# Token stage of a hybrid attention and MLP layer on one core: rope tables in one piece ahead of the token tiles, the first weights' low part on VectorE, norm vectors and rope rows loaded sooner

## What is computed

```python
def modulate(x, g, shift, scale):
    return rmsnorm(x, g) * (1.0 + scale) + shift

def project(h, w_in, g_q_a, w_uq, g_kv_a, w_ukv, g_mla_q, g_mla_k, g_swa_q, g_swa_k, rope):
    z = h @ w_in
    cq, ckv, kr, qs, ks, vs = jnp.split(z, offs, axis=-1)
    q_m = (rmsnorm(cq, g_q_a) @ w_uq).reshape(B, n, MLA_HEADS, MLA_QK)
    kv = (rmsnorm(ckv, g_kv_a) @ w_ukv).reshape(B, n, MLA_HEADS, MLA_NOPE + MLA_V)
    ...
    if rope is not None:
        q_m = jnp.concatenate([q_m[..., :MLA_NOPE], apply_rope(q_m[..., MLA_NOPE:], cos_m, sin_m)], axis=-1)
        k_m = jnp.concatenate([k_m[..., :MLA_NOPE], apply_rope(k_m[..., MLA_NOPE:], cos_m, sin_m)], axis=-1)
        q_s = apply_rope(q_s, cos_s, sin_s)
        k_s = apply_rope(k_s, cos_s, sin_s)
    return q_m, k_m, v_m, q_s, k_s, v_s
```

## Time and profile before

| | before |
|---|---|
| three runs, median (lowest to highest) | 1425.94 us (1423.24 to 1425.99) |
| the profiled execution's own time | 1423.98 us |
| its span in the trace | 1422.2 us |
| PE busy over the span | 95% |
| DVE, ACT, POOL busy over the span | 67%, 49%, 34% |
| mean granted TensorE clock | 0.989 of full speed |

### The profile page before, as it was taken

One profiled execution on the slowest core, in us unless ns is written; L12 is line 12 of the kernel. 1 busy time (PEld: TensorE's weight loads), 2 busy tenths in 40 slices (PEclk: granted clock), 3 DMA queues, 4 the chain that ended last, 5 costly groups with the idle time before them and its releaser, 6 DMA issues.

```text
span 1422.2 us, 18829 instructions
## 1 busy us (share of the span) xinstructions
PE 1354.3 (95%) x7274; PEld 1144.6 (80%) x7274; DVE 959.3 (67%) x1327; ACT 703.0 (49%) x1339; POOL 479.5 (34%) x295
## 2 busy tenths in 40 slices
PE   5799997999999999999999999999999999999969
PEld 1588886888788998998888888888888888888857
DVE  1888776888877877785774646557465656637477
ACT  2656655777778776972223424333233324323321
POOL 2666563000099992501002304132140503223060
PEclk9899999999999999999999999999999999999989
DMA  9465657900146556201123112121210212121003
GB/s 376 153 176 167 163 170 253 279 1 1 51 169 204 182 145 188 69 1 45 45 65 128 30 30 89 30 74 30 89 30 15 89 30 76 29 89 30 30 29 119
DMA packets 116969, 141.33 MB, mean 99 GB/s; under 512 B 7672, under 2 KB 98680, under 8 KB 114064
## 3 DMA queue, kind: packets, MB, share of 16 engines
q1 hardware_dynamic: 116624, 140.08, 31.5%
q0 software_dynamic: 256, 0.05, 0.0%
HBM read 108.37 MB, written 31.74 MB: 99 GB/s over the span
## 4 chain that ended last, share of the span: by engine, by line
PE 75%; DVE 11%; ACT 9%; DMA 2%; issue 2%; SPq 0%; DVEq 0%; ACTq 0%
PE f_ps L2024 24%; PE f_ps L2259 21%; PE a_ps L1381 7%; PE o_ps L1736 6%; PE a_ps L1397 6%; PE a_ps L1425 5%; ACT s_pr L1476 3%; PE t_ps L943 2%; ACT s_pT L1486 2%; PE t_ps L932 2%; DMA t_wm<-in_w_mod 1%; DVE s_nmx L1559 1%; PE t_ps L958 1%; ACT l_pr L1493 1%; DVE l_nb L1564 1%
## 5 line engine op out<-in xcount | busy, mean ns | idle before, releaser
L2024 PE MATMUL f_ps<-h,f_w 128*128 128x512 f32 x1536 | 357.9, 389 | 0.4 <-DVE h L1802 0.3
L2024 PEld LDWEIGHTS f_ps<-h,f_w 128*128 128x128 f32 x1536 | 288.1, 188 | 60.7 <-DVE h L1802 0.7
L2186 DVE TENSOR_TENSOR mix<-mix,f_ps 128x512 f32<-128x512 f32 x208 | 136.3, 683 | 149.6 <-PE f_ps L2259 149.6
L2067 POOL TENSOR_TENSOR f_w<-f_w,f_g 128x1024 f32<-128x1024 f32 x32 | 81.8, 2577 | 393.2 <-DMA f_w<-in_w_mlp 345.8
L2259 PE MATMUL f_ps<-f_bh,f_ah 128*128 128x512 f32 x448 | 175.4, 391 | 13.2 <-DVE mix L2186 13.1
L2259 PE MATMUL f_ps<-f_bh,f_al 128*128 128x512 f32 x448 | 175.0, 391 | 0.0
L2259 PE MATMUL f_ps<-f_bl,f_ah 128*128 128x512 f32 x448 | 175.0, 391 | 0.0
L2104 ACT ACTIVATE f_a<-f_ps 128x512 f32<-128x512 f32 x64 | 38.2, 597 | 254.7 <-PE f_ps L2024 254.7
L1573 DVE TENSOR_TENSOR l_pT<-a_ps,l_pT 128x512 fp32r<-128x512 f32 (+1 forms) x192 | 109.0, 594 | 53.0 <-ACT l_pT L1486 52.9
L1381 PE MATMUL a_ps<-l_k,l_q 96*128 96x512 f32 (+1 forms) x576 | 136.4, 366 | 0.5 <-DVE l_mo L1594 0.5
L943 PE MATMUL t_ps<-w_in,t_h 128*128 128x416 f32 (+2 forms) x600 | 123.6, 351 | 0.0
(11 more groups left out here) (212 smaller groups left out, 2355.2 us busy)
## 6 DMA issues: line engine op xcount, KB each, us to landing
l_wg<-in_w_mod SPq DMA_DIRECT2D x8, 2048.0 KB, 8.5
f_w1r<-in_w_mlp SPq DMA_DIRECT2D x32, 512.0 KB, 4.1
f_w<-in_w_mlp SPq DMA_DIRECT2D x16, 1024.0 KB, 5.0
t_wm<-in_w_mod SPq DMA_DIRECT2D x8, 1024.0 KB, 12.7
scratch_k<-t_kT SPq DMA_DIRECT2D x20, 384.0 KB, 4.3
l_k<-scratch_k SPq DMA_DIRECT2D x8, 960.0 KB, 9.7
scratch_q<-t_qT SPq DMA_DIRECT2D x16, 384.0 KB, 5.0
l_q<-scratch_q SPq DMA_DIRECT2D x8, 768.0 KB, 6.6
```

The costliest lines, as they stand in the source:

```text
L2024: last = nc.tensor.matmul(ps[:, b, :], w1[:, g % 2, w, k, :], h2[x][:, k, half * HB:(half + 1) * HB], start=(k == 0 and i == 0), stop=(k = ...
L2186: V.tensor_tensor(y, x, ps[:, bank_of(d, i, t), :].rearrange("p (k c) -> p k c", c=P), ALU.add).then_inc(added, 1)
```

## The change

Four things move. (1) On SP the two transfers of the norm vectors (`cols`, 2.5 KB, and `norms`, 160 KB) go ahead of the last two modulation blocks, and the rope rows (768 KB) go ahead of kv, r0 and r1. (2) On DVE the three small operations that scale the gains go from behind `scale_x(1)` to ahead of the bias. (3) The low part of a0 goes from POOL to DVE, ahead of `modulate_first`. (4) All four table blocks go ahead of POOL's loop.

```diff
@@ sync
         load_x(0)
+        sp.dma_start(cols[:, :], A["norm_cols"]).then_inc(gains, 16)
+        sp.dma_start(norms[:, :], A["norm_rows"]).then_inc(gains, 16)
         load_wm(KC - 2)
         load_wm(KC - 1)
         load_raw("a0")
         load_x(1)
         load_raw("a1")
-        sp.dma_start(cols[:, :], A["norm_cols"]).then_inc(gains, 16)
-        sp.dma_start(norms[:, :], A["norm_rows"]).then_inc(gains, 16)
+        sp.dma_start(rope[:, :, :], A["rope_rows"]).then_inc(rope_loaded, 16)
         load_raw("kv")
         load_raw("r0")
         load_raw("r1")
-        sp.dma_start(rope[:, :, :], A["rope_rows"]).then_inc(rope_loaded, 16)
@@ gpsimd
-        pool.wait_ge(w_hi, 1)
-        G.tensor_tensor(split_view("a0", 1), raw_view("a0"), split_view("a0", 0).bitcast(F32), ALU.subtract).then_inc(first_low, 1)
         pool.wait_ge(gains, 32)
         G.tensor_copy(tab[:, 0, 64:96], b_mk[:, NOPE:QK])
         link(G.tensor_copy(tab[:, 0, 256:320], b_sk))
+        pool.wait_ge(rope_loaded, 16)
+        pool.wait_ge(gains_scaled, 1)
+        build_table(0, 64, ROPE, b_mk[:, NOPE:QK])
+        build_table(2 * ROPE, 256, SD, b_sk)
+        build_table(2 * ROPE, 128, SD, b_sq)
+        build_table(0, 0, ROPE, b_mq[:, NOPE:QK])
         for i in range(NT + 1):
...
-            if i == 0:
-                pool.wait_ge(rope_loaded, 16)
-                build_table(0, 64, ROPE, b_mk[:, NOPE:QK])
-            if i == 1:
-                pool.wait_ge(gains_scaled, 1)
-                build_table(2 * ROPE, 256, SD, b_sk)
...
@@ vector
         inverse_x(0)
+        dve.wait_ge(gains, 32)
+        dve.wait_ge(cleared, 7)
+        V.scalar_tensor_tensor(out=g_qk[0:NOPE, :], in0=cols[0:NOPE, 3:4], scalar=MLA_SCALE, in1=cols[0:NOPE, 4:5],
+                               op0=ALU.mult, op1=ALU.mult)
+        V.tensor_scalar(b_mq, b_mq, MLA_SCALE, None, ALU.mult)
+        V.tensor_scalar(b_sq, b_sq, SWA_SCALE, None, ALU.mult).then_inc(gains_scaled, 1)
         dve.wait_ge(wm_used, KC)
         link(V.tensor_tensor(mo[:, :], ps[:, UB, :], bm, ALU.add))
         V.tensor_tensor(mo[:, :], mo[:, :], gm, ALU.mult).then_inc(mod_ready, 1)
+        dve.wait_ge(w_hi, 1)
+        V.tensor_tensor(split_view("a0", 1), raw_view("a0"), split_view("a0", 0).bitcast(F32), ALU.subtract).then_inc(first_low, 1)
         modulate_first()
         lo_fill("x0", 0)
         lo_fill("x1", 0)
         inverse_x(1)
         low_weights("a1")
         scale_x(1)
-        dve.wait_ge(gains, 32)
-        dve.wait_ge(cleared, 7)
...
-        V.tensor_scalar(b_mq, b_mq, MLA_SCALE, None, ALU.mult)
-        V.tensor_scalar(b_sq, b_sq, SWA_SCALE, None, ALU.mult).then_inc(gains_scaled, 1)
         low_weights("kv")
```

More of the change, by code:

```diff
@@ L467, in gpsimd @@
                 rotate_keys(i)
-            if i == 0:
-                pool.wait_ge(rope_loaded, 16)
-                build_table(0, 64, ROPE, b_mk[:, NOPE:QK])
-            if i == 1:
-                pool.wait_ge(gains_scaled, 1)
-                build_table(2 * ROPE, 256, SD, b_sk)
-                build_table(2 * ROPE, 128, SD, b_sq)
-                build_table(0, 0, ROPE, b_mq[:, NOPE:QK])
     def scalar():
@@ L837, in vector @@
         scale_x(1)
-        dve.wait_ge(gains, 32)
-        dve.wait_ge(cleared, 7)
-        V.scalar_tensor_tensor(out=g_qk[0:NOPE, :], in0=cols[0:NOPE, 3:4], scalar=MLA_SCALE, in1=cols[0:NOPE, 4:5],
-                               op0=ALU.mult, op1=ALU.mult)
-        V.tensor_scalar(b_mq, b_mq, MLA_SCALE, None, ALU.mult)
-        V.tensor_scalar(b_sq, b_sq, SWA_SCALE, None, ALU.mult).then_inc(gains_scaled, 1)
         low_weights("kv")
```

## The result

| | before | changed |
|---|---|---|
| median of thirteen runs (lowest to highest) | 1426.06 us (1423.24 to 1428.33) | 1428.75 us (1427.0 to 1430.58) |
| ratio of the runs, 95% interval | | 1.0021 (1.0012 to 1.0029) |
| the profiled execution's own time, span | 1423.98 us, 1422.2 us | 1429.06 us, 1427.2 us |
| mean granted TensorE clock of it | 0.989 | 0.983 |

The change makes the kernel slower by 2.7 us between the medians, 0.2%; the interval of the ratio is 1.7 to 4.1 us. That is a size that a measurement can just tell. The time is inside the forecast range and 0.75 us from the number.

A forecast was written before the change was run, and what follows sets the result against it. PE is busy 95%, but the first 80 us were taken as a relay between engines. +6.0 of delay less 1.5 coming back is +4.5; on a mean of 1424.8 that is 1429.3, forecast as 1429.5 us, range 1425.5 to 1432.5.

The forecast's parts named there:

- Tables: POOL: twelve table multiplications start at 34.0 us, 8.4 us alone, end at 48.2; `add_shift(1)` follows from about 48.3, 8.5 late.
- The turns: POOL and DVE: two-input DVE operations alternate with table operations, stopping them 6.6 us, less about 0.15 at each hand-over.
- x1 of tile 1 late by 6.0: PE: x1 of tile 1 follows x0 at about 51.6 instead of 45.71; everything behind it is 6.0 us late.
- What comes back: Turn 1: without tables on POOL, DVE's r3 and uq get 1.9 us shorter; 1.5 of it is handed on.
- The sum: Whole kernel: +6.0 for the delay less 1.5 coming back, +4.5 us.
- the forecast's own case: Whole kernel: slower by +3.2 to +6 us, chance 0.5.
- little change: PE at full clock in tile 1's up-projection and transposes saves 1.8 us, DVE 1.9: +2.3, 1427.1 us; chance 0.25.
- a0 on DVE, 1.55 us: DVE: a0's low part ahead of the modulation starts it 1.55 us later; bounds of the term 0.4 to 1.9.
- Transfers, 0.4 us: SP: 162.5 KB ahead of the last two modulation blocks delay them 0.4 us; bounds 0 to 1.
- Faster: POOL: DVE doesn't stop the tables, they end at 42.4, x1 isn't late: -1.7 us, 1423.1; chance 0.1.
- Slower still: PE idles from 45 to 50.7, then runs tile 1's first projection at half clock: +7 us, 1431.8; chance 0.15.
- a sign of being wrong: Whole trace: the two traces further apart or closer at 100 us than at the end would show the forecast wrong.

The follow-up runs named there:

- memsets_for_tables: The changed kernel with eighteen POOL memsets of 512 columns, which read nothing, in place of the twelve table multiplications (rope factors left out); ratio 1.0001 to the kernel before.
- tables_back: The changed kernel with the tables back in turns 0 and 1 of POOL's loop, transfers, gains and a0 as changed; ratio 1.0003 to the kernel before.
- a0_back_on_pool: The changed kernel with the low part of a0 back on POOL, ahead of the tables; ratio 1.0024 to the kernel before.
- before_again: The kernel before, unchanged, profiled and timed once more; ratio 1.0000.
- a0_alone: The kernel before with only the low part of a0 moved to DVE, ahead of `modulate_first`; ratio 0.9995.
- transfers_alone: The kernel before with only the changed kernel's order of transfers on SP; ratio 0.9998.
- spread_r0_r1: The kernel before with tables spread over POOL's turns 0 to 2, r0's low part later on DVE, r1's high part earlier on ACT; ratio 1.0002.

## Why the prediction was right, step by step

- **Tables.** Start predicted at 34.0, seen at 33.84; end at 48.2, seen at 47.52; `add_shift(1)` from 48.3, seen from 47.60. The turns were sized at 5.8 us net and took 5.3 (13.68 less 8.4); with nothing saved at the hand-overs they would have been 6.6. DVE's four operations came 1.8 us later than forecast (39.92 against 38.15) and still all fell on the tables, so the end of the tables hardly moved. That they are turns, and not a slower POOL, is shown by memsets_for_tables; that this is what costs the time, by tables_back and a0_back_on_pool.
- **x1 of tile 1 late by 6.0.** By the low part of r1, one link on, it was 5.66 against the profile of before. But against before_again, whose head is like that of nearly all executions, it is 55.11 - 51.21 = 3.90.
- **What comes back.** 1.5 us taken, 1.6 seen (5.66 at r1, 5.58 at tile 2's x0, 4.06 behind uq). At tile 2's variances the changed kernel has 92.04 (its row below) against 88.04 before, 4.0; and at tile 8's 236.07 against 232.03, the same 4.0: nothing is added or lost in between.
- **The sum.** +4.5 predicted; +2.7 between the medians. That is below the +3.2 with which the forecast's own case began, and nearer to the +2.3 of the rival "little change": the time was forecast well, the difference less well. The step that failed is the base on which all others stand, that the profiled execution's head is the usual one ("all sums are in the time of the profiled execution"). In the usual head PE is at half clock and everything behind the modulation is some 1.7 us later anyway (tile 2's variances at 89.74 against 88.04), while the tables, which start with the landing of the rope rows and not with PE, are not. The delay of `add_shift(1)` is a difference of the two, so it shrinks by about that: 4.5 - 1.76 = 2.74. That this meets the 2.7 so closely is chance. Between the two first profiles the delay at tile 2 was 4.0 and not 4.5, and against before_again it is 92.04 - 89.74 = 2.30; both 2.3 and 2.7 lie in the interval of the ratio. The number 1429.5 came out close because the base had also been taken low, at 1424.8 instead of 1426.06: two errors of opposite sign, 1.8 and 1.3 us, and in so far luck.
- **a0 on DVE, 1.55 us.** (By its own terms it is 1.64: 30.06 + 0.4 + 1.89 - 30.71.) Mis-sized: nothing in the usual head by the trace of a0_alone, where the modulation starts at the same time; its ratio, 0.9995 with at most +0.7 us, agrees. The lower bound given, 0.4, was still too high by that trace, though the times can't tell 0.4 from 0. It is never paid in the changed kernel in any case, since the tables end later.
- **Transfers, 0.4 us.** 0.48 seen in the trace, and tile 2's variances at 90.37 against 89.74 in before_again; in the time it is too small to be told (transfers_alone, 0.9998, at most +1.3 us). In the changed kernel the tables' delay covers what it costs on PE and DVE; it reaches the sum only by way of the rope rows.
- **Rivals.** "Faster" had POOL and DVE not stopping each other; memsets_for_tables is that case, and even it gives 1.0001 and not 0.9988: with the usual head, r0 (3.91) meets `add_shift(1)` instead of kv, and the stop only moves. "Little change" gave +2.3, nearest to the +2.7 measured, and had the cause wrong: the clock made the difference, but in the head and in the kernel before. The full clock that it wanted at tile 1's up-projection didn't come: four transposes take 1.09 us and the up-projection 2.91 in the changed kernel (64.23, 67.18) as before (58.65, 61.59). "Slower still" did not come: PE's transposes at 50.09 took 1.94 us for eight, more than the 0.66 for four of the full clock, but its first projection of tile 1 took 4.67 us, against 4.81 before, and so ran at full clock.

The two rows on which the comparison at tile 2 and at tile 8 rests, of the changed kernel:

```profile
92.04 0.69 DVE L738 TENSOR_REDUCE t_stn<-t_sqk 128x8 f32<-128x512 f32 x1 [0.70 <-ACT t_sqk L576]
...
236.07 0.69 DVE L738 TENSOR_REDUCE t_stn<-t_sqk 128x8 f32<-128x512 f32 x1 [0.40 <-ACT t_sqk L576]
```

Between the two first profiles the difference grows once more, from 4.0 us at 236 to 5.0 at the end of the span, which the prediction had named as a sign of being wrong. It is the clock again: from 240 to 270 us its mean is 0.96 in the first profile of before, 0.83 in the changed kernel and 0.81 in before_again. Against before_again the difference doesn't grow, 2.3 us at 236 and 1.9 at the end. So the first profile had been spared twice. What stays open is why, and with it how much of the missing 1.8 us is the base: one second profile and the timed executions' mean clocks stand for "the usual head".

## What to carry to other kernels

An engine that waits for 12 us is not free: ask which instruction stands behind the block that you put there, when that instruction is wanted, and what the other engine does in the same microseconds. Work that reads SBUF on GpSimd costs its length plus the length of every two-input VectorE operation that falls into it, and costs VectorE too; here 8.4 us became 13.7. And before working a difference out from one profile, look whether its clock in that stretch is that of the other executions; here a second profile of the same kernel would have brought the forecast of the difference from +4.5 to about +2.7.

## What the runs showed of the hardware

- A VectorE operation with one small SBUF input can be stopped as well. L798 of the changed kernel adds a constant to 128x2 numbers; it takes 0.15 us by itself and took 1.98 us beside `add_shift(1)`, and it ended with that operation, at 49.97. The prediction had counted only operations with two inputs. In spread_r0_r1 two more small operations on `t_stn` (the second also reads `t_eps`) took 0.55 and 0.76 us beside the tables, instead of 0.17 and 0.23.
- The memsets on POOL stopped no VectorE operation with two SBUF inputs (18 of 512 columns in 8.70 us in memsets_for_tables; the low part of a1 and `scale_x(1)` on DVE beside them took 1.89 and 1.28, as alone).
- The granted clock in the head differs between executions of one program: 1.00 from 22 to 36 us in the first profile of before, 0.60 in the second, with the same transfers and much the same waits of PE for them, 0.5 to 1.0 us, ahead of the fall.
